# One diffusion layer with 32 experts: projection banks, a moved norm buffer, and expert 0's rows by one-hot products

## The reference

```
mod  = silu(cond) @ w_ada + b_ada          # shift1, scale1, gate1, shift2, scale2, gate2
h    = LN(x) * (1 + scale1) + shift1
merged = sigmoid gates of h * (attention branch) + sigmoid gates of h * (gated linear attention branch)
x    = LN(alpha * x + gate1 * (merged @ w_out)) * ln1_g + ln1_b
h2   = LN(x) * (1 + scale2) + shift2
# router: best of 4 groups, best 2 of the 8 experts in it, softmax weights
y    = sum over the 2 experts e of w_e * (silu(h2 @ gate_e) * (h2 @ up_e)) @ down_e
out  = LN(alpha * x + gate2 * y) * ln2_g + ln2_b
```

## Time and profile before

| | |
|---|---|
| runs, us | 685.9, 683.66, 684.82 (median 684.82) |
| profiled execution, us | 686.07 |
| its span from first to last instruction, us | 684.2 |
| mean granted TensorE clock | 0.983 |
| PE, DVE, ACT, POOL busy | 92%, 42%, 15%, 17% |
| DMA | 176.66 MB, mean 258 GB/s |

### The profile page before, as it was taken

How to read it: one execution, slowest core, us unless ns; L and a number is a source line. 1 busy time by engine, 2 the same in 40 slices (tenths; PEclk the granted TensorE clock), 3 DMA queues, 4 the chain that set the end, 5 groups by cost and what they waited for, 6 DMA issues and landing times.

```text
span 684.2 us, 8540 instructions
## 1 busy us (share of the span) xinstructions
PE 626.5 (92%) x3361; PEld 346.1 (51%) x3361; DVE 288.6 (42%) x627; ACT 104.0 (15%) x220; POOL 115.6 (17%) x116
## 2 busy tenths in 40 slices
PE   6999998998998999999999899999999888878994
PEld 3553354644355556565554355666565544444541
DVE  4322633136756774401323875133343322222356
ACT  2001542210022223240000011211111111111000
POOL 4000000010300000000000221433433322221102
PEclk9999989999999999999999999999999999999998
DMA  9997737344130311227997069699999999999862
GB/s 335 377 329 266 245 124 247 124 130 179 23 125 0 124 53 71 54 71 204 362 405 318 31 250 366 246 416 415 415 415 415 415 415 417 413 416 418 362 246 92
DMA packets 56201, 176.66 MB, mean 258 GB/s; under 512 B 10644, under 2 KB 12724, under 8 KB 44512
## 3 DMA queue, kind: packets, MB, share of 16 engines
q1 hardware_dynamic: 39264, 143.34, 54.1%
q10 hardware_dynamic: 11152, 24.47, 10.2%
q0 software_dynamic: 5744, 8.28, 3.5%
HBM read 174.58 MB, written 11.96 MB: 273 GB/s over the span
## 4 chain that ended last, share of the span: by engine, by line
PE 58%; DMA 22%; DVE 11%; issue 3%; SPq 2%; POOL 2%; ACT 1%; ACTq 0%; DVEq 0%; POOLq 0%
PE bank L1606 10%; DMA Y<-exp_w_up 9%; PE bank L1876 8%; PE bank L1595 7%; PE bank L1790 6%; PE bank L1777 6%; DMA X<-exp_w_up 4%; DMA W<-exp_w_up 4%; PE bank L1559 3%; PE bank L1885 3%; PE bank L1519 2%; SPq L484 2%; DVE X L1040 1%; DMA Y<-w_ada 1%; DMA X<-pair_rows 1%
## 5 line engine op out<-in xcount | busy, mean ns | idle before, releaser
L1876 PE MATMUL bank<-X,Y 128*64 128x256 f32 x672 | 80.4, 389 | 12.7 <-DMA X<-exp_w_up 11.9
L1606 PE MATMUL bank<-Y,W 128*128 128x384 f32 x256 | 86.6, 492 | 0.0
L1876 PEld LDWEIGHTS bank<-X,Y 128*64 128x64 f32 x672 | 50.1, 134 | 47.9 <-DMA X<-exp_w_up 19.3
L688 POOL TENSOR_TENSOR rstd<-ss,cst 128x1 f32<-128x1 f32 (+3 forms) x21 | 22.5, 1073 | 304.8 <-DVE ss L821 304.8
L1595 PE MATMUL bank<-W,Y 128*128 128x512 f32 x144 | 67.1, 621 | 0.0
L1606 PEld LDWEIGHTS bank<-Y,W 128*128 128x128 f32 x256 | 47.4, 190 | 36.0 <-issue 5.6
L1205 DVE COPY abias<-bank 128x128 f32<-128x128 f32 x32 | 9.3, 291 | 116.2 <-PE bank L1909 116.2
L731 POOL DMA_INDIRECT Y<-h_rows,gidx x32 | 41.3, 1291 | 93.3 <-PE bank L1850 88.7
L1790 PE MATMUL bank<-X,Y 128*128 128x512 f32 x96 | 43.4, 613 | 2.6 <-issue 2.3
L1595 PEld LDWEIGHTS bank<-W,Y 128*128 128x128 f32 x144 | 27.9, 199 | 32.7 <-issue 32.7
L1876 PE MATMUL bank<-W,Y 128*64 128x256 f32 (+1 forms) x320 | 37.0, 345 | 7.5 <-DMA W<-exp_w_up 3.8
(11 more groups left out here) (234 smaller groups left out, 748.5 us busy)
## 6 DMA issues: line engine op xcount, KB each, us to landing
X<-exp_w_gate SPq DMA_DIRECT2D x22, 1024.0 KB, 22.4
X<-exp_w_up SPq DMA_DIRECT2D x22, 1024.0 KB, 26.2
X<-exp_w_down SPq DMA_DIRECT2D x22, 1024.0 KB, 26.8
Y<-w_ada ACTq DMA_DIRECT2D x16, 1024.0 KB, 8.2
W<-w_in SPq DMA_DIRECT2D x7, 2048.0 KB, 9.2
W<-exp_w_gate SPq DMA_DIRECT2D x10, 1024.0 KB, 22.1
W<-exp_w_up SPq DMA_DIRECT2D x5, 1024.0 KB, 26.5
W<-exp_w_down SPq DMA_DIRECT2D x5, 1024.0 KB, 29.5
```

The costliest lines, as they stand in the source:

```text
L688: nc.gpsimd.tensor_tensor(rstd[:, 0:n], ss[:, 0:n], const("mhalf", 0, n), ALU.pow)\
L1606: ins = mm(bank[:, 0:TOKENS], w[:, k, c * P:(c + 1) * P], hT[:, :, k, :], start=k == 0, stop=k == KT - 1)
L1876: ins = mm(bank[hh * 64:hh * 64 + 64, a:b], x_[:, c, h * 64:h * 64 + 64], rhs(hh), start=k == 0 and a == 0, stop=k == KT - 1, skip_group_c ...
```

## The change

Three things are changed. First, the projection has its own ring of four banks (0, 1, 4, 5), and the last tile's second half is cut into two pieces of 256 columns, so that there are seven pieces; the last tile's statistics are taken in four chunks of 256. The first norm's `ln1` lies in `PTr` (all four parts), and its loads are issued behind the modulation loads; the loads of gate2, which use part of `PTr`, come after the last h2. The second norm's intermediate value goes to where `ln1` was. Second, expert 0's 64 rows are no longer gathered: DVE makes one one-hot per tile from the rank bank, PE multiplies them with the h2 rows in `xr`, for each half row, into bank 1, and ACT copies the result into `G`. POOL's first gathers are those of experts 1 to 3. SP's last load ahead (expert 5, up) waits for that product, as its buffer is where `xr` lies. Third, of the fill products one after the count stays, and those before the transposes of expert 0 are gone.

```diff
-FILL_NORM, FILL_ROUTER, FILL_RANK, FILL_GATHER = 4, 5, 2, 4
+FILL_NORM, FILL_ROUTER, FILL_RANK = 4, 5, 1
...
-    jobs += [("wo", n, i) for i in range(TILES) for n in range(2)] + [("router",)]
     return jobs
+WO_COLS = {(n, i): slice(n * HALF, (n + 1) * HALF) for i in range(TILES) for n in range(2)}
+WO_COLS[1, LAST_TILE] = slice(HALF, HALF + HALF // 2)
+WO_COLS[2, LAST_TILE] = slice(HALF + HALF // 2, 2 * HALF)
+def last_jobs():
+    return [("wo",) + job for job in WO_COLS] + [("router",)]
...
-        ln1 = lambda j: Y1[:, j, 0, :]
-        ln2 = ln1
+        ln1 = lambda j: PTr[:, 2 * j:2 * j + 2, :].rearrange("p a n -> p (a n)")
+        ln2 = lambda j: Y1[:, j, 0, :]
...
+        last = Banks((0, 1, 4, 5), banks, full, read, last_jobs(), uses)
+        expert0 = Banks((1,), banks, full, read, [("rows",)], uses)
...
@@ SP @@
-            side.wait_full(sp, "hT", TILES - 1, 1)
+            expert0.wait_full(sp, "rows")
             load_part(sp, "exp_w_up", 1, PARTED, PARTED, ew_in[PARTED])
...
@@ POOL @@
-            for n in range(NSLOT):
+            for n in range(1, NSLOT):
                 gather_rows(n)
...
@@ DVE, projection @@
+                chunk = HALF if i < LAST_TILE else HALF // 2
+                for n in range(2 if i < LAST_TILE else 3):
+                    cols = WO_COLS[n, i]
...
-                    step(half_stats(x1(i), n))
+                    for c in range(cols.start, cols.stop, chunk):
+                        ins = V.bn_stats(stats[:, c // chunk, :], x1(i)[:, c:c + chunk])
+                    step(ins)
...
-                normed = PTr[:, 0:2, :].rearrange("p a n -> p (a n)")
+                normed = Y1[:, 0, 0, :]
...
@@ DVE, behind the rank bank @@
             bank = side.wait_full(dve, "rank")
+            for i in range(TILES):
+                ins = V.tensor_scalar(first_slots[:, i, :], const("iota_rows", 0, SLOT_ROWS), bank[:, i * NE:i * NE + 1],
+                                      both[:, i, 0:1], ALU.is_equal, ALU.mult)
+            ins.then_inc(S["onehot_ready"], FIRST_SLOTS)
...
@@ ACT @@
-            for o in range(2):
-                for st in range(2):
-                    act.dma_start(g2r[o * SLOT_ROWS:(o + 1) * SLOT_ROWS, st, :],
...
+            for j in range(2):
+                act.dma_start(ln1(j), (T["ln1_g"], T["ln1_b"])[j].to_broadcast([P, D])).then_inc(S["ln1_in"], 16)
             main.wait_full(act, "br", KT - 1, 1)
...
-            act.wait_ge(S["merged_ready"], KT)
-            for j in range(2):
-                act.dma_start(ln1(j), (T["ln1_g"], T["ln1_b"])[j].to_broadcast([P, D])).then_inc(S["ln1_in"], 16)
...
             act.wait_ge(S["h2_ready"], TILES)
+            for o in range(2):
+                for st in range(2):
+                    act.dma_start(g2r[o * SLOT_ROWS:(o + 1) * SLOT_ROWS, st, :],
...
+            bank = expert0.wait_full(act, "rows")
+            expert0.was_read(A_(G[:, 0, :], bank[:, :], ACT.Copy), "rows")
             act.wait_ge(S["xTe_full"], 1)
             tokens(0, S["xTe_ready"])
...
@@ PE, projection @@
+            for (n, i), cols in WO_COLS.items():
+                h = cols.start // HALF
+                at, width = cols.start - h * HALF, cols.stop - cols.start
...
+                    ins = mm(bank[:, 0:width], mT[:, i, k, :], w[:, k, at:at + width], start=k == 0, stop=k == KT - 1)
...
@@ PE, behind the count @@
             keep_busy(FILL_RANK)
+            pe.wait_ge(S["onehot_ready"], FIRST_SLOTS)
+            bank = expert0.claim(pe, "rows")
+            for i in range(TILES):
+                for h in range(2):
+                    ins = mm(bank[h * SLOT_ROWS:(h + 1) * SLOT_ROWS, :], first_slots[:, i, :],
+                             xr(i)[:, h * HALF:(h + 1) * HALF], start=i == 0, stop=i == TILES - 1, skip_group_check=True)
+            expert0.filled(ins, "rows")
...
             def next_tokens(n):
-                pe.wait_ge(g_in[n % NSLOT], (n // NSLOT + 1) * 16)
+                if n:
+                    pe.wait_ge(g_in[n % NSLOT], (n // NSLOT + (n % NSLOT > 0)) * 16)
+                else:
+                    expert0.wait_read(pe, "rows")
...
             index_tables(0)
-            keep_busy(FILL_GATHER)
             next_tokens(0)
```

More of the change, by code:

```diff
@@ L51 @@
 LAST = 2
+LAST_TILE = TILES - 1
 CHECK = 28
@@ L272, in program @@
         modc = sb("modc", [P, 2 * KT, 2])
-        stats = sb("stats", [P, 2, 6])
+        stats = sb("stats", [P, 4, 6])
         mv = sb("mv", [P, 2])
@@ L618, in _ @@
             load_part(sp, "exp_w_gate", 0, PARTED, PARTED, ew_in[PARTED])
-            for n in range(2):
-                main.wait_full(sp, "wo", n, TILES - 1)
+            for n in range(3):
+                last.wait_full(sp, "wo", n, LAST_TILE)
             load_down(sp, 1, 1, ed_in[1])
@@ L836, in half_stats, with norm_affine @@
                 return V.bn_stats(stats[:, g, :], src[:, g * HALF:(g + 1) * HALF])
-            def norm_affine(src, dst, gain, shift, have_stats=False, halves=None):
+            def norm_affine(src, dst, gain, shift, have_stats=0, halves=None):
                 if not have_stats:
@@ L842, in norm_affine @@
                     step(half_stats(src, 1))
-                step(V.bn_aggr(mv[:, :], stats[:, :, :].rearrange("p a b -> p (a b)")))
+                chunks = have_stats or 2
+                step(V.bn_aggr(mv[:, :], stats[:, 0:chunks, :].rearrange("p a b -> p (a b)")))
                 ask_power(ss[:, 0:1], mv[:, 1:2], 1.0, EPS)
@@ L1080, in _ @@
             for i in range(TILES):
-                for n in range(2):
-                    cols = slice(n * HALF, (n + 1) * HALF)
+                chunk = HALF if i < LAST_TILE else HALF // 2
+                for n in range(2 if i < LAST_TILE else 3):
+                    cols = WO_COLS[n, i]
                     dve.wait_ge(S["mod_in"], 16 * 6)
[L1085 to L1088, removed]
+                    bank = last.wait_full(dve, "wo", n, i)
+                    ins = V.tensor_tensor(x1(i)[:, cols], bank[:, 0:cols.stop - cols.start], g1b[:, stream(i), cols],
+                                          ALU.mult)
+                    last.was_read(ins, "wo", n, i)
+                    last.wait_read(dve, "wo", n, i)
                     dve.wait_ge(xr_in[i], 16)
@@ L1091, in _ @@
                                                 ALU.mult, ALU.add))
-                    step(half_stats(x1(i), n))
+                    for c in range(cols.start, cols.stop, chunk):
+                        ins = V.bn_stats(stats[:, c // chunk, :], x1(i)[:, c:c + chunk])
+                    step(ins)
                 dve.wait_ge(S["ln1_in"], 32)
-                step(norm_affine(x1(i), x1(i), ln1(0), ln1(1), have_stats=True))
-                normed = PTr[:, 0:2, :].rearrange("p a n -> p (a n)")
+                step(norm_affine(x1(i), x1(i), ln1(0), ln1(1), have_stats=D // chunk))
+                normed = Y1[:, 0, 0, :]
                 tell(norm_affine(x1(i), normed, sc2b[:, stream(i), :], sh2b[:, stream(i), :], halves=h2_halves(i)),
                      "h2_ready")
-            bank = main.wait_full(dve, "router")
+            bank = last.wait_full(dve, "router")
             ins = V.tensor_tensor(logit[:, :, :],
@@ L1104, in _ @@
                                   rbias[:, :].unsqueeze(1).to_broadcast([P, TILES, GROUPS + NE]), ALU.add)
-            main.was_read(ins, "router")
-            main.wait_read(dve, "router")
+            last.was_read(ins, "router")
+            last.wait_read(dve, "router")
             def wide(a, n):
@@ L1451, in _ @@
             act.wait_ge(S["h2_ready"], TILES)
+            for o in range(2):
+                for st in range(2):
+                    act.dma_start(g2r[o * SLOT_ROWS:(o + 1) * SLOT_ROWS, st, :],
+                                  mod_d[st:st + 1, (6 + o) * HALF:(7 + o) * HALF].to_broadcast([SLOT_ROWS, HALF]))\
+                        .then_inc(S["gate2_in"], 16)
             for j in range(2):
@@ L1782, in _ @@
                     used(pe.nop(), "br", c // 4)
[L1783 to L1791, removed]
+            for (n, i), cols in WO_COLS.items():
+                h = cols.start // HALF
+                at, width = cols.start - h * HALF, cols.stop - cols.start
+                pe.wait_ge(wout_in[h], 16)
+                w = wout[h].rearrange("p (k n) -> p k n", k=KT)
+                bank = last.claim(pe, "wo", n, i)
+                for k in range(KT):
+                    pe.wait_ge(S["merged_ready"], k + 1)
+                    ins = mm(bank[:, 0:width], mT[:, i, k, :], w[:, k, at:at + width], start=k == 0, stop=k == KT - 1)
+                last.filled(ins, "wo", n, i)
             def second_transposes(i):
@@ L1802, in _ @@
                 if i == 0:
-                    bank = main.claim(pe, "router")
+                    bank = last.claim(pe, "router")
                 for g in range(2):
@@ L1808, in _ @@
```

(12 more changed lines are left out.)

8 lines of the change are left out of this document (4 added, 4 removed).

## The result

| | before | after |
|---|---|---|
| median, us | 685.05 (681.02 to 687.82, 14 runs) | 678.89 (676.3 to 680.95, 14 runs) |
| ratio | 1 | 0.9921, 95% interval 0.9903 to 0.9938 |
| profiled span, us | 684.2 | 677.1 |
| mean granted clock | 0.983 | 0.985 |

The change is faster by 6.2 us in the medians, and by 4.2 to 6.6 us by the interval of the ratio. The same kernel was timed twice more, in the experiments: ratio 0.9931 (0.9904 to 0.9958) and 0.9934 (0.9910 to 0.9957). The three together speak for about 5 us.

A forecast was written before the change was run, and what follows sets the result against it. The prediction took one stream of expert weights, started by its first refill after expert 0's gate-and-up product, to bound the kernel. 4.7 + 2.3 - 0.8 = 6.2 us off 684.82 gave 678.6 us, range 676.0 to 682.4.

The forecast's parts named there:

- What bounds the kernel: Last two hundred microseconds: one weight stream through six buffers, ending at its first refill's time plus bytes over rate.
- Part 1: Projection on four banks, norm loads earlier, last piece halved: gain 4.7 us, between 3.6 and 5.2.
- The 32 narrow matmuls: Projection's halved last piece, 256 columns wide: 0.225 us each, 7.2 us in all; half of a 512 is 0.217.
- Part 2: Expert 0's rows by one-hot product instead of gather: transposes begin at 426.6 instead of 428.92, gain 2.3 us.
- The 12 instructions: Expert 0's six one-hot products on PE, 64 stationary columns by 512: 2.9 us in all.
- The three small one-hots: DVE makes them from the rank bank: at most 0.22 us each, 0.6 us, ending under the one fill product left.
- such a drain: TensorE drain at switches between whole-array and half-array products: 0 by the trace, 0.7 us together by the skill's rule.
- Expert 1's gather: Behind expert 0's product: lands near 430.6, with expert 1's transposes at 431.9; index path 1.7 us later.
- Part 3: Zeroing scatters and a gather now share DMA engines with the weight stream: loss 0.8 us, between 0 and 2.15.
- The rival of the falling clock: PE drops to 1.2 GHz ahead of the one-hot products: 9.4 us more, 688.0 us; chance 0.06.
- the step that adds the parts: Each microsecond expert 0's product ends earlier comes off the end: 4.7 + 2.3 - 0.8 = 6.2 us.
- the low end of the range: Whole kernel: better bounds (5.2 + 2.5, no loss in the stream), less 1.1 for runs' spread: 676.0 us.

The follow-up runs named there:

- ln1_late: The changed kernel with the first norm's two loads issued late, where they were before; 684.26 us in one run.
- two_banks: The changed kernel with the projection on two banks, as before; 678.71 us in one run.
- p2_only: The kernel before plus only expert 0's one-hot product, with the fill taken out; projection as before; 682.39 us, ratio 0.9978 to before.
- again: The changed kernel without an edit, timed and profiled a second time; 678.92 us, ratio 0.9931 to before.
- again_2: The changed kernel without an edit, third time; 679.98 us, ratio 0.9934 to before.
- router6: The changed kernel with one more fill product ahead of the rank product; 678.74 us, ratio 0.9925 to before.
- zero_router6: The changed kernel with an early plain store of zeros for the zeroing scatters and one more fill product before the rank product; 678.34 us, ratio 0.9918.
- the five profiles above: Five of ten profiles with the one-hot product, in which PE stands still for expert 1's gather, 0.22 to 2.47 us.
- zero_early: The changed kernel with the two zeroing scatters replaced by one plain store of zeros after the attention; 678.09 us, ratio 0.9920 to before.
- p1_only: The changed kernel with the one-hot product and fill removal undone, leaving only the projection edits; 685.39 us, ratio 1.0021 to before.
- p1_clear: Projection edits alone, with expert 5's up load and the second output norm's loads held until gathered rows are read; 683.47 us, ratio 1.0000.

## Why the prediction was right, and where it was not

- **What bounds the kernel** held: in all profiles the last weights land 201.5 to 204.2 us after the first refill, and what follows them is 47.3 to 48.0 us.
- **Part 1** (from 48.0 to 43.2, counted as 4.7): measured 43.3 in every profile that has all of it. The cause given, a chain of late norm loads and too few banks, is what `ln1_late` and `two_banks` show, and an operation on 256 columns takes 0.42 to 0.43 us on DVE, as taken. The 32 narrow matmuls took about 0.21 us each (41.48 us for all 112, less 80 at 0.433), below the lower bound of 0.217. But the size of the gain was read from one profile of before. In `p2_only` the old projection took 45.83: 1.7 us less because the clock did not fall after the standstill, and 0.5 less because the standstill was shorter. So by these two profiles the gain lies between 2.5 and 4.7.
- **Part 2** (2.3 us): 2.6 to 2.8 at the full clock (`again`, `again_2`), 1.0 where PE ran at the low one, as in the profile after. The 12 instructions were set at 2.9 and took 2.79 in `again`. The three small one-hots were set at 0.6 and took 0.77 to 1.18, hidden; in `router6` and `zero_router6` they took 1.5, and PE waited 0.44 us for them. No drain between whole-array and half-array products is visible: in `again` the next product follows at 416.02, without a gap (the ends of matmuls are modelled, so a short one would not show). The Trainium skill, TensorEngine Tiling (Array Packing), section Tiling Modes, names such a drain; by these rows it costs nothing that can be seen.
- **Expert 1's gather** was said to land near 430.6, 1.3 us before it is needed, at the 3.10 us of the earlier trace rows. In `again` the index tables end 1.8 us later after the rank product than before, about the 1.7 named. But in the five profiles above the gather took 4.22 to 6.47 us beside loads, and PE waited for it. The price of the gather is the term that was too low. In four of the five the wait cost nothing that can be seen at the end, in `zero_router6` the stream ran dry.
- **Part 3** (0.8 us within 0 to 2.15): the stream is 1.0 to 1.3 us longer in the three profiles of the changed kernel, 1.5 in `p2_only`. The size was a little low; that the zeroing scatters are the cause rests on one profile.
- **The rival of the falling clock** was half right. In the index part it happened in the profile after and in one more of eight, for part of the way, at a cost of 1.6 us and not of 9.4. Elsewhere it came too: in `again_2` ten fill instructions ahead of the rank product took 5.96 us (4.54 in `p2_only`), in `zero_early` and `zero_router6` expert 1's product was slow. That the removed fill is the cause is not shown: in `p1_only`, where all of it is there, the four instructions behind the count took 2.95 us (timeline of PE) instead of the 1.96 of the earlier trace rows. The Trainium skill, TensorE: Matmul & The Clock Gate, part 1, has the low clock as the default that activity releases. The runs agree as far as longer standstills go (3.03 us in `p1_only`), but after the same standstill of 1.06 us ahead of the rank product the clock fell in the profile after (0.76 from 414 to 421) and stayed at 1.00 in `again` (412 to 418).
- **What failed is the step that adds the parts**, "every microsecond by which expert 0's product ends earlier should therefore come off the end", read as if each part brought its own share. Part 1 alone brings nothing (ratio 1.0021), part 2 alone 1.5 us, both together about 5: at least 2.9 by the lowest interval, where the two alone add up to at most 2.8. By the profile of `p1_only`, while the gather stands in the path, part 1 only moves it in among the loads ahead. The one-hot product is what lets part 1 through. The sum was right because both parts were made; the prediction did not name this dependence.

The medians' 6.2 us agree with the forecast of 6.2 better than the reasons deserve: by the profiles, 2.5 to 4.7, 1.0 to 2.8 and a loss of 1.0 to 1.5 make 2 to 6.5, and the three timings of the changed kernel lie at 3.8 to 6.2 in the medians, 4.5 to 5.4 by the ratios. The agreement to a tenth is luck. The 2.5 us that the low end of the range takes for part 2 are not worked out in the prediction.

## What to carry to other kernels

Where a stream of loads ends the kernel, work out what releases its first refill and count every edit by that moment, then ask of each transfer on the way which other loads it will run beside once it comes earlier. Taking a small gather out of that path can be worth more than its own latency. And read a stage's length from several profiles before taking a low clock in it as part of the cost.

## What the runs showed of the hardware that was not expected

- A 64-row gather took 3.10 us (before) and 3.12 us (`p1_clear`) while the DMA engines were 0.42 and 0.15 busy, and 4.22 to 6.47 us in six other profiles while they were 0.66 to 0.83 busy.
- The clock behind a standstill is not the same each time: in the projection 0.63 after 2.32 us in one profile and 1.00 after 1.84 us in another; ahead of the rank product 0.76 and 1.00 after the same 1.06 us; after 3.03 us in `p1_only` 0.72 over the next eight.
- The stages ahead of the projection, whose compute no edit touches, varied by 5 us (349.6 to 354.7), as much as the change is worth, and by 4.5 us in three profiles of one and the same kernel.
